# The mixing phases of a two-layer encoder with stationary weight blocks and moving tokens, and the second norm folded into its neighbours

## What is computed

```python
for i in range(2):
    h = rmsnorm(x) * g                      # norm_a, norm_b
    q, k, v, gate = split(h @ w_in, 4)
    o = attention_i(q, k, v)                # 0: differential, 1: stick-breaking
    x = x + (o * silu(gate)) @ w_out        # k and v are outputs too
    x = x + sigmoid(x @ w_gate[i]) * (p[i] @ w_proj[i])     # p has 256 features
y = rmsnorm(x) * g_final
```

## Time and profile before

| | |
|---|---|
| median of 3 runs | 2196.36 us (2194.26 to 2197.1) |
| the profiled execution | 2200.13 us, span 2198.3 us |
| busy: PE / DVE / ACT / GpSimd | 88% / 56% / 46% / 9% |
| mean granted TensorE clock | 0.941 of 2.4 GHz |
| mix_a, first to last matmul | 771.3 to 1021.0 us |
| last matmul of mix_a to first of the stick layer | 1020.9 to 1079.2 us |
| mix_b, first to last matmul | 1927.1 to 2184.1 us |

### The profile page before, as it was taken

How to read it: one execution, slowest core, us unless ns; L and a number is a source line. 1 busy time by engine, 2 the same in 40 slices (tenths; PEclk the granted TensorE clock), 3 DMA queues, 4 the chain that set the end, 5 groups by cost and what they waited for, 6 DMA issues and landing times. The chain is left out here.

```text
span 2198.3 us, 34267 instructions
## 1 busy us (share of the span) xinstructions
PE 1943.0 (88%) x10820; PEld 1567.1 (71%) x10820; DVE 1234.1 (56%) x2491; ACT 1001.0 (46%) x2248; POOL 198.9 (9%) x420
## 2 busy tenths in 40 slices
PE   2999999999999499994589999999999999589995
PEld 2878878878778378872477877777787877378873
DVE  4456455455564443332448687777868676743332
ACT  4445454454454432222436455564646555433322
POOL 0111111111111000000001010111101010100000
PEclk7999999999999799997599999999999999699997
DMA  3121112111112242111310101110110101251110
GB/s 126 49 60 50 45 44 64 47 44 53 58 34 64 85 152 71 62 37 51 117 31 24 58 19 60 41 49 29 53 54 23 58 19 45 75 172 62 62 37 22
DMA packets 129570, 126.78 MB, mean 58 GB/s; under 512 B 11888, under 2 KB 113840, under 8 KB 129520
## 3 DMA queue, kind: packets, MB, share of 16 engines
q1 hardware_dynamic: 127120, 117.50, 17.5%
q10 hardware_dynamic: 2400, 8.65, 1.0%
HBM read 91.52 MB, written 34.60 MB: 57 GB/s over the span
## 5 line engine op out<-in xcount | busy, mean ns | idle before, releaser
L103 PE MATMUL lb_pj<-lb_w_high,h_high 128*128 128x384 f32 (+1 forms) x576 | 203.5, 353 | 23.3 <-DVE lb_w_low L1229 13.2
L103 PE MATMUL la_pj<-la_w_high,h_high 128*128 128x384 f32 (+1 forms) x576 | 208.5, 362 | 12.2 <-DVE la_w_low L550 12.2
L103 PE MATMUL la_pj<-la_w_low,h_high 128*128 128x384 f32 (+1 forms) x576 | 196.3, 341 | 0.0
L103 PE MATMUL lb_pj<-lb_w_low,h_high 128*128 128x384 f32 (+1 forms) x576 | 195.6, 340 | 0.0
L103 PE MATMUL lb_pj<-lb_w_high,h_low 128*128 128x384 f32 (+1 forms) x576 | 195.5, 339 | 0.0
L103 PE MATMUL la_pj<-la_w_high,h_low 128*128 128x384 f32 (+1 forms) x576 | 195.4, 339 | 0.0
L1401 POOL TENSOR_TENSOR lb_o<-lb_o,lb_keep 128x512 f32<-128x512 f32 (+3 forms) x80 | 77.3, 967 | 948.2 <-ACT lb_keep L1114 948.2
L1090 ACT ACTIVATE lb_m<-lb_m 128x512 f32<-128x512 f32 (+4 forms) x200 | 98.8, 521 | 137.5 <-DVE lb_m L1250 136.8
L1263 DVE TENSOR_TENSOR lb_s<-lb_sc,lb_m 128x512 f32<-128x512 f32 (+4 forms) x200 | 110.2, 551 | 48.0 <-ACT lb_m L1095 47.9
L403 ACT ACTIVATE la_p<-la_sc,la_nm 128x128 f32<-128x128 f32 (+5 forms) x144 | 106.0, 738 | 58.0 <-DVE la_nm L584 56.1
L103 PEld LDWEIGHTS lb_pj<-lb_w_high,h_high 128*128 128x128 f32 (+1 forms) x576 | 104.5, 181 | 33.8 <-issue 14.3
(11 more groups left out here) (285 smaller groups left out, 4844.9 us busy)
## 6 DMA issues: line engine op xcount, KB each, us to landing
stage_a<-in_a_w_in SPq DMA_DIRECT2D x60, 192.0 KB, 3.3
stage_b<-in_b_w_in SPq DMA_DIRECT2D x60, 192.0 KB, 2.5
norm_a_xt<-in_x SPq DMA_DIRECT2D x8, 512.0 KB, 3.3
stage_a<-in_a_w_in SPq DMA_DIRECT2D x16, 256.0 KB, 3.8
out_ak<-la_tok SPq DMA_DIRECT2D x8, 512.0 KB, 3.3
out_av<-la_tok SPq DMA_DIRECT2D x8, 512.0 KB, 4.0
o_t<-la_o SPq DMA_DIRECT2D x16, 256.0 KB, 2.9
stage_a<-in_a_w_out SPq DMA_DIRECT2D x8, 512.0 KB, 4.5
```

Source lines behind the costliest of these rows:

```text
L103: last = pe.matmul(out, x, y, start=start and n == 0, stop=stop and n == 2, **kw)
```

## The change

- **Layout.** Both mix phases work with features on partitions and tokens in the free dimension. A visit holds one block of 128 output features: 8 visits for w_out, then 8 for w_gate and w_proj. Its weights (128 x 8 or 10 blocks of 128) are stationary, and the tokens move in `PIECES` of 384, 384 and 288. x, x1 and x2 stay transposed; `x_mid` becomes (8, 128, 1056).
- **Weights.** No full set in SBUF: two slots, each split on ACT and DVE a visit ahead, loaded by SP as 128-column strips (rows of 512 bytes).
- **Last head group of a layer.** `h` is filled with the branch blocks read back from `o_t` and split (seven blocks), the eighth straight from SBUF (`split_own`); it is no longer stored. After the seventh split the first two weight strips of the mix are loaded into `stage`, now one buffer for the whole kernel.
- **mix_a.** x is loaded in strips and transposed on TensorE into the accumulator of the out product. x2 = x1 high + x1 low + gate term is made on GpSimd and stored by SP. Its square is summed over the blocks (ACT, GpSimd), and x2 times the norm's gain is split straight into `h`. At the end matmuls with a constant 1/1024 give the mean square; Ln and Exp make 1/rms along the tokens in two layouts. norm_b is gone.
- **stick_layer.** 1/rms is applied late: as a per-token scale in the ACT copies of q, k, v, and to the raw gate by an extra product on GpSimd (`gate_norm`) before the clamp.
- **mix_b.** The gate visits come in two passes: pieces 0 and 1 over blocks 0 to 7, then piece 2 over blocks 7 to 0 (six of them loaded and split again). In the second pass token tiles 0 to 5 are transposed back, one a visit, normed and stored by SP; tiles 6 to 8 follow at the end.

The core of the diff (semaphore tables, buffer declarations, and the mirrored edits in the stick layer are left out):

```diff
+PIECES = [(0, 3 * P), (3 * P, 3 * P), (6 * P, 2 * P + DEC)]
+LOADED = GROUPS - 1
@@ diff_layer, SP (the stick layer alike)
-                    for k in range(OUT_SLOTS, KT):
-                        sp.wait_ge(S["out_low"], k - OUT_SLOTS + 1 + 1)
-                        sp.dma_start(out_raw(k), w_out[k * P:(k + 1) * P, :]).then_inc(S[f"out_loaded{k}"], 16)
+                    for k in range(2, LOADED):
+                        load_block(k)
+                    load_first_out()
...
+            def load_first_out():
+                sp.wait_ge(S["block_low"], LOADED + 1)
+                for dst, src in first_blocks(w_out, stage):
+                    sp.dma_start(dst, src).then_inc(S["first_out"], 16)
...
+            sp.wait_ge(S["first_out"], 32 + 1)
@@ stick_layer
-                act.activation(tok[0:n, t, 0:P], pj[0:n, t % 2, 0:P], ACT.Copy, scale=DH ** -0.5)
+                act.activation(tok[0:n, t, 0:P], pj[0:n, t % 2, 0:P], ACT.Copy, scale=by_token(t, 0))
...
-                    dve.wait_ge(S["g_raw"], at.next("g_raw"))
+                    dve.wait_ge(S["g_normed"], at.next("g_normed"))
...
+                def gate_norm(c):
+                    g = gate[:, gate_cols(c)]
+                    pool.wait_ge(S["g_raw"], at.next("g_raw"))
+                    pool.tensor_tensor(g, g, norm["row"][:, gate_cols(c)], ALU.mult).then_inc(S["g_normed"], 1)
@@ mix_phase
+    PASSES = [[0, 1], [2]] if final else [[0, 1, 2]]
+    VISITS = [("out", n, n) for n in range(KT)] + [("gate", n, KT + n) for n in range(KT)]
...
+    SUMS = 3
@@ SP
+            for i, (kind, n, m) in enumerate(VISITS):
+                for j in splits_at[i + 2] if i + 2 < len(VISITS) else ():
+                    load_w(j)
...
+                elif not final and i > KT:
+                    for v in units_at[i - 1]:
+                        store(v)
+                for t in tiles_at[i]:
+                    if t > 0:
+                        send(t - 1)
@@ ACT
+            for i, (kind, n, m) in enumerate(VISITS):
+                for j in splits_at[i]:
+                    split_high(j)
...
+                    else:
+                        sigmoid_log(u)
+                        if not final and u > 0:
+                            square(u - 1)
+                            next_high(u - 1)
+                        sigmoid(u)
+                for t in tiles_at[i]:
+                    statistics(t)
@@ DVE
+                for j in splits_at[i]:
+                    split_low(j)
...
+                        clamp(u)
+                        if not final and u > 0:
+                            next_low(u - 1)
+                        soft(u)
+                        product(u)
+                for t in tiles_at[i]:
+                    normed(t)
@@ GpSimd
+            def whole(v):
...
+                if not final and v >= SUMS:
+                    pool.wait_ge(S["h_low"], v - SUMS + 1)
+                    pool.wait_ge(S["squared"], v - SUMS + 1)
+                    pool.wait_ge(S[f"stored{v % SUMS}"], 16 * (v // SUMS))
+                pool.tensor_tensor(x2_of(v), x1_of(0, unit).bitcast(F32), x1_of(1, unit).bitcast(F32), ALU.add).then_inc(S["sum"], 1)
...
+            for v in range(len(GATE_UNITS)):
+                whole(v)
+                add(v)
+                if not final and v > 0:
+                    accumulate(v - 1)
@@ TensorE
+            def product(out, weights, data, k, c, start, stop):
+                return three(pe, out, [x[:, k[0], :] for x in weights], [x[:, k[1], cols(c)] for x in data], start, stop,
+                             skip_group_check=True)
...
+            def gate_unit(v, m):
...
+                if v >= 2:
+                    pe.wait_ge(S["prod"], v - 1)
+                for k in range(PT):
+                    product(pp_bank(v), w[slot[m]], pt, (KT + k, k), c, k == 0, k == PT - 1)
                 for k in range(KT):
+                    last = product(gt_bank(v), w[slot[m]], x1, (k, k), c, k == 0, k == KT - 1)
+                last.then_inc(S["gt"], 1)
...
+                for c in range(NP):
+                    pe.matmul(yb[:, c, 0:PIECES[c][1]], mean[:, :], acc[:, cols(c)], start=True, stop=True)
@@ build
-            norm_phase(nc, top, "norm_b", x_mid, A["b_norm_g"], ident, h, first_weights(A["b_w_in"], stage))
```

More of the change, by code:

```diff
@@ L649, in body @@
                         split_gate(r + 1, GATE_WEIGHTS_AT[j])
[L650 to L652 removed]
+                    if not more and j in BLOCKS_AT:
+                        for k in BLOCKS_AT[j]:
+                            split_block(k)
                 normalize(1)
@@ L957, in stick_layer @@
         tile_cols = lambda t: slice(t * P, t * P + TILES[t][1])
+        chunk = lambda c: slice(CHUNKS[c][0], CHUNKS[c][0] + CHUNKS[c][1])
+        by_token = lambda t, part: norm["token"][0:TILES[t][1], part, t:t + 1]
         def bank(s):
@@ L1194, in body @@
                             next_tokens(5)
+                if not more:
+                    for n, c in enumerate(STORED):
+                        act.wait_ge(S["o_ready"], at.nth("o_ready", n + 1))
+                        act.activation(h[0][:, LOADED, chunk(c)], o[:, chunk(c)], ACT.Copy).then_inc(S["block_high"], 1)
             for k in range(KT):
@@ L1772, in _, with split_high @@
-            act.wait_ge(S["stored"], done("stored", NT))
+            act.wait_ge(S["fill"], 1)
+            def split_high(m):
+                if m >= 2:
+                    act.wait_ge(S[f"w_loaded{slot[m]}"], arrived(m))
+                    i = last_visit(before(m))
+                    act.wait_ge(S["y" if VISITS[i][0] == "out" else "gt"], through(i))
+                high = w[slot[m]][0]
+                ins = act.activation(high[:, 0:KT, :], raw(m), ACT.Copy)
+                if BLOCKS[m][0] == "gate":
+                    ins = act.activation(high[:, KT:, :], raw_proj[:, slot[m]], ACT.Copy)
+                ins.then_inc(S["w_high"], 1)
@@ new lines, in sigmoid, with square @@
+            def sigmoid(v):
+                e = sig_of(v)
+                act.wait_ge(S["soft"], v + 1)
+                act.activation(e, e, ACT.Exp, scale=-1.0).then_inc(S["sig"], 1)
+            def square(v):
+                n, c = GATE_UNITS[v]
+                act.wait_ge(S["x2"], v + 1)
+                if n == 0:
+                    out = acc[:, cols(c)]
+                else:
+                    out = sq[:, v % 2, 0:PIECES[c][1]]
+                    if summed(v - 2) > 0:
+                        act.wait_ge(S["acc"], summed(v - 2))
+                act.activation(out, x2_of(v), ACT.Square).then_inc(S["squared"], 1)
@@ new lines, in _ @@
+            if final:
+                for t in range(6, NT + 1):
+                    statistics(t)
+            else:
+                square(len(GATE_UNITS) - 1)
+                next_high(len(GATE_UNITS) - 1)
+                act.wait_ge(S["mean"], 1)
+                out, by_token = norm["row"], norm["token"]
+                for c in range(NP):
+                    act.activation(out[:, cols(c)], yb[:, c, 0:PIECES[c][1]], ACT.Ln, bias=eps[:, 0:1]).then_inc(S["mean_log"], 1)
+                act.activation(by_token[:, 1, :], yb[:, 3, 0:NT + 1], ACT.Ln, bias=eps[:, 0:1]).then_inc(S["mean_log"], 1)
+                act.wait_ge(S["mean_log"], NP + 1)
+                act.activation(by_token[:, 1, :], by_token[:, 1, :], ACT.Exp, scale=-0.5).then_inc(S["rstd"], 1)
+                act.activation(out[:, :], out[:, :], ACT.Exp, scale=-0.5)
+                act.wait_ge(S["rstd"], 1)
+                act.activation(by_token[:, 0, :], by_token[:, 1, :], ACT.Copy, scale=DH ** -0.5)
@@ L1844, in _ @@
         @block.tensor
         def _(pe):
-            def product(out, n, parts, weights, blocks, split_first=None):
-                for half in range(2):
-                    for k in range(blocks):
-                        if split_first is not None and half == 0:
-                            pe.wait_ge(S["w_low"], split_first + k + 1 + 1)
-                        last = three(pe, out[0:n, half, :], [x[:, k, 0:n] for x in parts],
-                                     [weights(part, k)[:, half * 512:(half + 1) * 512] for part in range(2)],
-                                     k == 0, k == blocks - 1)
-                return last
@@ new lines, in _ @@
+            if final:
+                for t in range(6, NT + 1):
+                    turn(t)
+            else:
+                pe.wait_ge(S["acc"], NP * (KT - 1))
+                for c in range(NP):
+                    pe.matmul(yb[:, c, 0:PIECES[c][1]], mean[:, :], acc[:, cols(c)], start=True, stop=True)
+                for t in range(NT + 1):
+                    last = pe.matmul(yb[:, 3, t:t + 1], acc[:, t * P:(t + 1) * P], mean[:, 0:1], start=True, stop=True,
+                                     skip_group_check=True)
+                last.then_inc(S["mean"], 1)
```

656 lines of the change are left out of this document (388 added, 268 removed).

## The result

The changed kernel takes 2176.01 us (median of 4 runs, 2175.48 to 2181.56), the kernel before beside it 2196.73 (4 runs, 2194.26 to 2200.07): ratio 0.991, interval 0.989 to 0.993. It is faster, as predicted, but by 21 us (0.9%) and not by 66: 2176 lies above the whole range of 2092 to 2170. The profiled execution has a span of 2174.1 us against 2198.3.

A forecast was written before the change was run, and what follows sets the result against it. TensorE, busy 88% of the span, was taken as the bound in both mix phases. Terms of -2, 0, -32, 0, -7 and -25 gave -66 us, so 2130 us was predicted, range 2092 to 2170.

The forecast's parts named there:

- Stick layer: Stick layer: 24 extra GpSimd products before the gate's clamp are covered; 0 to +10 us, taken as 0.
- Before mix_a: 26.9 us stretch ahead of mix_a: store, reload and waits go, two 512 KB loads come; -2 us, between -5 and +3.
- Before mix_b: 16.1 us stretch ahead of mix_b: store and reload of o go, two 512 KB loads come; -7 us, between -10 and -2.
- Matmuls of a piece: Both mix phases: matmul time close to proportional to columns, 0.174 us at 384 and 0.132 at 288.
- mix_a: First mix phase: gate part bound by the DVE and ACT chain, 145 us; in sum 249 against 249.7, nothing won.
- two upper ends: mix_a's gate part: 155 us at most; collisions charged in full, some 3 us more a visit, also called the upper end.
- rival A: Both mix phases: chains stay hidden and TensorE bounds them, mix_a's gate part 118 us; 2093 us in all, chance 0.15.
- The term for the store: mix_a's gate part: GpSimd's addition waits for an earlier store, so a Square is about 1.5 us late.
- Border to the stick layer: From mix_a's last matmul to the first projection: norm removed, short tail added; 26 us for 58.3, so -32.
- mix_b: Second mix phase with the end: second gate pass in series, 7.1 us a visit; 246 us against 271, so -25.
- Rival B: Collisions and store waits cost more in mix_a, mix_b's second pass, stick-layer gates and borders: 2165 us, chance 0.21.
- Rival C: Mix gate parts: TensorE waits in every visit and its granted clock falls to 1.2 GHz; up to 2292 us, chance 0.05.

The follow-up runs named there:

- the last kernel: Changed kernel with the gate's norm product on DVE ahead of the splits, 25 start credits given by GpSimd, earlier mix_a stores, 111 idle instructions: 2126.43 us, ratio 0.968.

## Why the prediction was wrong in size and right in sign

**The step that failed is "Stick layer".** It read: "24 extra GpSimd products ... The clamp is queued in the next step anyway and GpSimd is idle 88% of that stage; if the cover fails, DVE waits under 1 us each time ...: 0 to +10, I take 0." It was +45, for two reasons: a cost of the products that the step put at nothing, and a wait at DVE's jump back that it did not have at all.

- 14 us are the products themselves (14.2 in the stick layer, 17 by the medians of whole executions, whose intervals are some 3.6 us wide to each side). I asked who waits for them, and the answer was right in effect: the wait costs nothing (the kernel in which the clamp doesn't wait is as slow). I did not ask what runs beside them. Both of DVE's operands of a weight split lie in SBUF, and the earlier trace rows had shown 0.87 us for 0.29 in such a case. The rule of the Trainium skill ("SBUF — State Buffer", Who interferes with whom) that I charged to mix_a applied to the stick layer as well, and there it met steps on the path. An idle share of 88% says nothing of the moments at which the work falls. Each split is only some 0.75 us late; over 7 groups with two such splits this makes 10.4 us, as in the sums over all splits (48.4 for 38.0), and the slower clock behind them (0.53 in the window shown) is the likely rest: without the products PE is busy 7.1 us less.
- 26 us come from DVE's loop lying across one block of instructions more. The loop is 365 instructions long in both kernels. In the changed one it starts 18 places later and the blocks lie some 20 places lower; by the table either shift alone would take it across a fourth block. It was in no rival either. The Trainium skill ("Runtime: NRT & Kernel Launch", Instruction fetch mechanics) says that a taken branch whose target is outside the blocks held forces a fetch before execution goes on. The trace agrees in kind, with 2.4 us a jump; it differs in the block, 8 KB packets 128 instructions apart where the page has 16 KiB and 256, and a loop of 365 over three such blocks ran without a fetch.

Of the 45 us in the stick layer 26 + 14 are 40 when one of the two is taken away; with both taken away, in the last kernel, all but 2.5 are gone. What is between these two figures stays unexplained. That last kernel without its earlier stores (4.5 us by the medians) would take about 2131, beside the 2130 of the prediction. Such a close meeting is partly luck: mix_a came out 3.2 us below its term and the border 3.6 above.

**The other terms, one by one.**
- Before mix_a: -2 predicted, -2.3 measured. Before mix_b: -7 and -6.9. No run tells the two loads apart from the rest of these stretches.
- Matmuls of a piece: the columns' proportion held, 0.132 us predicted for 288 columns, 0.133 measured:

```profile
1010.08 0.29 PE L105 MATMUL mix_a_g<-mix_a_x_high,mix_a_w_high 128*128 128x288 f32 x1
...
1011.15 0.29 PE L105 MATMUL mix_a_g<-mix_a_x_low,mix_a_w_high 128*128 128x288 f32 x1
```

(eight steps in 1.07 us).
- mix_a: 249 predicted, 245.8 measured. The gate part ran as told, bound by the chain between DVE and ACT: the six visits in the middle took 17.3 to 19.8 us, mean 18.5, against 19.3. (The prediction's two upper ends don't agree: 3 us more in each of six visits would give 163, not 155. Neither was reached.) Each of its named causes is in the trace:

```profile
956.08 1.02 POOL L2040 TENSOR_TENSOR mix_a_xs<-mix_a_x_high,mix_a_x_low 128x384 f32<-128x384 f32 x1 [6.04 <-DMA x_mid<-mix_a_xs]
...
959.29 1.04 DVE L1992 SCALAR_TENSOR_TENSOR h_low<-mix_a_xs,mix_a_gain,h_high 128x384 fp32r<-128x384 f32 x1 [3.99 <-ACT h_high L1888]
...
968.55 1.23 DVE L1954 TENSOR_TENSOR mix_a_w_low<-mix_a_raw_proj,mix_a_w_high 128x256 fp32r<-128x256 f32 x1
```

GpSimd waits for the store, and two DVE steps take 1.04 and 1.23 us that took 0.62 and 0.41 where nothing ran beside them. That "nothing is won" there was right, and rival A (chains hidden, visits of 14.4 us) is refuted; only without the fold do the visits come near it (14.6 to 16.5). The term for the store was nearly twice too large (0.9 us a visit for 1.5).
- Border to the stick layer: 26 predicted, 29.6 measured. The mean's matmuls took 7.5 us where I took 5 (outside my 2 to 6), and the unit's chain ahead of them 8.2 for 6.8:

```profile
1019.64 3.89 PE L2134 MATMUL mix_a_y<-mix_a_acc,mix_a_mean 128*128 128x384 f32 x6 [8.20 <-POOL mix_a_acc L2054]
1023.32 3.84 PE L2136 MATMUL mix_a_y<-mix_a_mean,mix_a_acc 128*128 128x1 f32 x18
```

Each of the 3 + 9 fp32 matmuls stands in the trace twice, and the nine of a single column cost as much as three of up to 384. Ln and Exp took 2.9 for 3.3.
- Scales from SBUF: 0.09 us more on each of 144 copies, 13 us of ACT where the term had -1 to +3, but hidden: 0 on the path, as taken.
- mix_b: 246 predicted, 247.2 measured; a visit of the second pass 6.70 us against 7.1, in series as told:

```profile
2123.11 1.23 DVE L1952 TENSOR_TENSOR mix_b_w_low<-stage,mix_b_w_high 128x1024 fp32r<-128x1024 f32 x1
...
2129.81 1.23 DVE L1952 TENSOR_TENSOR mix_b_w_low<-stage,mix_b_w_high 128x1024 fp32r<-128x1024 f32 x1
```

- Rival B had the direction of the miss (collisions cost more), with 8 us for the gates in the stick layer; it was 14 there. Rival C saw that a stage with waits gets a slower clock, but looked for it in the mix phases, where the clock stayed at 0.98 and 0.96; it came in the stick layer.

## To carry to other kernels

Work put on an idle engine has two prices: who waits for it, and what runs at the same moment and gets slower beside it; read the second from the timelines of both engines at that place, not from the share of idle time. When straight code takes the place of a loop, or any instructions are added ahead of a loop that is on the path, look for "issue" waits at its jump back and for instruction packets in the DMA view of one pass: zero packets a pass is the aim, and some idle instructions elsewhere can be worth over 1% (86 of them gave 26 of 2176 us here). Judge a change with that effect taken out, otherwise its sign can be decided by where its code happens to lie.

## What the runs showed of the hardware that was not expected

- A loop of 365 instructions on DVE costs nothing at its jump back while it lies within three blocks of 128 instructions, and waits 2.4 to 3.3 us a jump when it reaches into a fourth; then 5 packets of 8 KB a pass are fetched. My reading is that four blocks are held and that reaching the fourth sends for a fifth in place of the first; the runs show the packets and where they fall, not what is held. Why the blocks lie some 20 instructions apart between the kernel before and the changed one, while all variants of the changed one share them, stays open.
- A short wait was paid for twice. Behind the 5 us in which PE was busy 1.96 the granted clock was 0.72, behind those with 2.86 it was 0.53, near the lower of its two levels (1.2 of 2.4 GHz), in a layer that before had 0.98; of the 26 us of the jumps 14.3 are the waits themselves, and PE's busy time for the same 4752 matmuls is 17.2 us longer with them than without; the two overlap.
